# Second output projection of a two-layer decoder step, turned from feature rows to token rows

## What is computed

```python
# pool_mixer, layer 1; y is (tokens, 4096)
y = mixed * scale * silu(z)
out = y @ w_out                 # (tokens, 4096) @ (4096, 2048)
# trunk
hp = hp + op; hs = hs + os_     # residual
y_prompt = rmsnorm(hp, final_norm_w); y_sample = rmsnorm(hs, final_norm_w)
def rmsnorm(x, w):
    return x * rsqrt(mean(x * x, axis=-1) + 1e-6) * w
```

## Time and profile before

| | |
|---|---|
| timed runs | 2078.85, 2078.79, 2073.24 us; median 2078.79 |
| profiled execution | 2073.52 us |
| its span, first to last instruction | 2071.8 us |
| TensorE busy in the span | 99% |
| VectorE, ScalarE, GpSimd busy | 62%, 45%, 8% |
| mean granted TensorE clock | 0.995 of 2.4 GHz |
| HBM traffic | 283.85 MB read, 27.25 MB written |

### The profile page before, as it was taken

One profiled execution on the slowest core, in us unless ns is written; L12 is line 12 of the kernel. 1 busy time (PEld: TensorE's weight loads), 2 busy tenths in 40 slices (PEclk: granted clock), 3 DMA queues, 4 the chain that ended last, 5 costly groups with the idle time before them and its releaser, 6 DMA issues.

```text
span 2071.8 us, 51652 instructions
## 1 busy us (share of the span) xinstructions
PE 2045.3 (99%) x19451; PEld 1961.4 (95%) x19451; DVE 1277.5 (62%) x2245; ACT 936.8 (45%) x2013; POOL 168.7 (8%) x354
## 2 busy tenths in 40 slices
PE   8999999999999999999999999999999999999997
PEld 7999999999999999999899999999999999999997
DVE  5767677777677777767754445545546656644444
ACT  5555555565555555455543343333333333433333
POOL 4111111011111011111000010000000000000000
PEclk9999999999999999999999999999999999999999
DMA  6544555554455554455554445444454444454452
GB/s 201 168 132 134 162 153 153 152 145 122 140 162 162 148 151 135 124 155 156 160 168 152 143 142 182 144 158 149 148 165 151 147 147 158 158 162 144 141 161 73
DMA packets 381227, 311.13 MB, mean 150 GB/s; under 512 B 20041, under 2 KB 377114, under 8 KB 380570
## 3 DMA queue, kind: packets, MB, share of 16 engines
q1 hardware_dynamic: 379290, 306.30, 48.7%
q10 hardware_dynamic: 1872, 3.96, 0.6%
HBM read 283.85 MB, written 27.25 MB: 150 GB/s over the span
## 4 chain that ended last, share of the span: by engine, by line
PE 92%; DVE 6%; issue 1%; ACT 1%; DMA 0%; POOL 0%; DVEq 0%; ACTq 0%; POOLq 0%; SPq 0%
PE ps L298 27%; PE ps L299 25%; PE ps L300 25%; PE ps L1221 10%; DVE s_s L1154 2%; PE ps L1371 2%; DVE wlo L289 1%; DVE silu L1016 1%; DVE silu L1014 1%; DVE amat L1164 1%; PE ps L1411 0%; PE ps L1345 0%; DVE xlo L1008 0%; DMA ht<-ht_save 0%; DVE xlo L893 0%
## 5 line engine op out<-in xcount | busy, mean ns | idle before, releaser
L298 PE MATMUL ps<-xhi,whi 128*128 128x320 f32 x3072 | 983.3, 320 | 7.4 <-DVE xlo L1008 3.5
L300 PE MATMUL ps<-xhi,wlo 128*128 128x320 f32 x3072 | 949.1, 309 | 0.0
L299 PE MATMUL ps<-xlo,whi 128*128 128x320 f32 x3072 | 948.8, 309 | 0.0
L289 DVE TENSOR_TENSOR wlo<-wraw,whi 128x1024 fp32r<-128x1024 f32 (+1 forms) x484 | 596.0, 1252 | 236.6 <-ACT whi L284 234.1
L284 ACT ACTIVATE whi<-wraw 128x1024 fp32r<-128x1024 f32 (+1 forms) x484 | 498.1, 1049 | 318.7 <-PE ps L300 287.9
L298 PEld LDWEIGHTS ps<-xhi,whi 128*128 128x128 f32 x3072 | 576.9, 188 | 32.0 <-issue 17.4
L299 PEld LDWEIGHTS ps<-xlo,whi 128*128 128x128 f32 x3072 | 577.4, 188 | 0.9
L300 PEld LDWEIGHTS ps<-xhi,wlo 128*128 128x128 f32 x3072 | 576.6, 188 | 0.0
L298 PE MATMUL ps<-bhi,whi 128*128 128x320 f32 x512 | 157.6, 308 | 0.0
L299 PE MATMUL ps<-blo,whi 128*128 128x320 f32 x512 | 157.6, 308 | 0.0
L300 PE MATMUL ps<-bhi,wlo 128*128 128x320 f32 x512 | 157.6, 308 | 0.0
(11 more groups left out here) (342 smaller groups left out, 2077.4 us busy)
## 6 DMA issues: line engine op xcount, KB each, us to landing
wraw<-in_delta_w_in_dram SPq DMA_DIRECT2D x384, 256.0 KB, 3.0
wraw<-in_pool_w_in_dram SPq DMA_DIRECT2D x256, 256.0 KB, 3.0
wraw<-in_delta_w_out_dram SPq DMA_DIRECT2D x128, 256.0 KB, 3.3
wraw<-in_pool_w_out_dram SPq DMA_DIRECT2D x128, 256.0 KB, 3.2
s_s<-in_state_delta_dram SPq DMA_DIRECT2D x32, 512.0 KB, 6.3
out_dram<-s_s SPq DMA_DIRECT2D x32, 512.0 KB, 4.2
wraw<-in_pool_w_group_dram SPq DMA_DIRECT2D x64, 256.0 KB, 3.2
dec<-gc_rows SPq DMA_DIRECT2D x16, 320.0 KB, 4.1
```

The source lines that it names most:

```text
L289: nc.vector.tensor_tensor(wlo[:, slot, 0:width], wraw[:, slot, 0:width], whi[:, slot, 0:width].bitcast(F32), ALU.subtract).then_inc(E("w_l ...
L298: mm(o, whi[:, slot, w], hi[:, k_x, :], start=first, stop=False)
L299: mm(o, whi[:, slot, w], lo[:, k_x, :], start=False, stop=False)
L300: done = mm(o, wlo[:, slot, w], hi[:, k_x, :], start=False, stop=last)
```

## The change

The second output projection is done with the roles exchanged. The tokens of `branch` are stationary (128 at a time) and the weights move, 512 output columns at a time, so the result comes in token rows. There are three groups of tokens: 128 and 128 of the prompt, and the 64 of the samples. The samples' high and low parts stand side by side in one stationary tile of 128 columns (`rows_s`), so this group takes two matmuls instead of three; its low x low product comes along, and the two halves of the result (64 partitions each) are added by VectorE. A piece is now 2 input tiles x 512 columns (`two_rows`), and there are 8 steps of 8 pieces: 2 halves of the input x 4 blocks of 512 columns, with three banks a step, two sets in turn (4, 5, 6 and 0, 1, 2). In the first four steps TensorE also turns `ht` into token rows, by 12 groups of 4 transposes into banks 7 and 3 after the first three pieces of a step, and ScalarE copies them into `hrow` and `hrow_c`; VectorE adds each step's product to these rows. Squares are summed along the row by ScalarE's accumulator, one column a group and block. `final_norm_w` is loaded as one row spread over all partitions (`wrow`), and each finished block of 512 columns but the last is multiplied by it into `yrow` (`weigh`). In the last step the last four pieces are worked off group by group; after each group come its add, square, root, reciprocal, a scaling of 1536 columns on ScalarE (for the samples 896, the rest on VectorE) and of the last 512 on VectorE, and two stores. GpSimd has no part in the stage.

The steps of `out_sp`, `out_act`, `out_dve` and `out_pe` for r = 2 are taken out; for r = 1 they stay as they were. At the end of `mix` two lines change, and the last four loads of it fetch pieces of the new form:

```diff
-                    sc.activation(xhi[:, 4 * ch:4 * ch + 4, :], branch[:, 4 * ch:4 * ch + 4, :], ACT.Copy).then_inc(E("b_hi"), 1)
+                    rows_hi_part(0, ch)
...
-                    v.tensor_tensor(xlo[:, 4 * jb:4 * jb + 4, :], branch[:, 4 * jb:4 * jb + 4, :],
-                                    xhi[:, 4 * jb:4 * jb + 4, :].bitcast(F32), ALU.subtract).then_inc(E("b_lo"), 1)
+                    rows_lo_part(0, jb)
...
-            out_sp(sp, 2, OUT_B, pw_out)
+            rows_sp(sp)
...
-            out_pool(pool, 2)
...
-            out_act(act, 2, OUT_B, J_OUT_B)
+            rows_act(act)
...
-            out_dve(dve, 2, OUT_B, J_OUT_B)
+            rows_dve(dve)
...
-            out_pe(pe, 2, OUT_B, J_OUT_B)
+            rows_pe(pe)
```

The new functions:

```diff
+    F0 = J_OUT_B // 2 + 1
+    STEPS = 8
+    ROWS = ((P, 0), (P, 1), (64, 2))
+
+    ROW_SIDES = ((rows_hi0, rows_lo0, rows_s0), (rows_hi1, rows_lo1, rows_s1))
+
+    def rows_hi_part(half, ch):
+
+        hi, lo, both = ROW_SIDES[half]
+        k, src = slice(4 * ch, 4 * ch + 4), branch[:, KT * half + 4 * ch:KT * half + 4 * ch + 4, :]
+        nc.scalar.activation(hi[:, k, :], src[:, :, 0:256], ACT.Copy)
+        nc.scalar.activation(both[:, k, 0:64], src[:, :, 256:T], ACT.Copy).then_inc(E("b_hi"), 1)
+
+    def rows_lo_part(half, ch):
+
+        hi, lo, both = ROW_SIDES[half]
+        k, src = slice(4 * ch, 4 * ch + 4), branch[:, KT * half + 4 * ch:KT * half + 4 * ch + 4, :]
+        nc.vector.tensor_tensor(lo[:, k, :], src[:, :, 0:256], hi[:, k, :].bitcast(F32), ALU.subtract)
+        nc.vector.tensor_tensor(both[:, k, 64:P], src[:, :, 256:T], both[:, k, 0:64].bitcast(F32), ALU.subtract
+                                ).then_inc(E("b_lo"), 1)
+
+    def step_banks(t):
+
+        return (4, 5, 6) if t % 2 == 0 else (0, 1, 2)
+
+    def row_chunk(g, s):
+
+        c = slice(512 * s, 512 * s + 512)
+        return hrow[:, g, c] if g < 2 else hrow_c[s // 2][0:64, 512 * (s % 2):512 * (s % 2) + 512]
+
+    def sq_col(g, s):
+        return small[0:64 if g == 2 else P, 16 + 4 * g + s:17 + 4 * g + s]
+
+    def rows_sp(sp):
+        for t in range(STEPS):
+            half, s = t // 4, t % 4
+            for pc in range(8):
+                n = 8 * t + pc
+                if n < 4:
+                    continue
+                load(sp, OUT_B + n, pc % 4, two_rows(pc % 4, KT * half + 2 * pc, 512 * s))
+            if t == 4:
+                sp.wait_ge(E("w_used"), OUT_B + 32)
+                sp.dma_start(wrow[:], final_norm_w.partition_broadcast(P)).then_inc(E("rows_in"), 16)
+        y_s = y_sample.rearrange("b s c -> (b s) c")
+        for rows, g in ROWS:
+            y = y_prompt[0, P * g:P * g + P, :] if g < 2 else y_s
+            sp.wait_ge(E("dve_tiles"), len(BY_DVE) + g + 1)
+            sp.dma_start(y[:, 1536:DM], row_chunk(g, 3)).then_inc(E("rows_out"), 16)
+            sp.wait_ge(E("act_tiles"), len(BY_ACT) + g + 1)
+            sp.dma_start(y[:, 0:1536], yrow[0:rows, g, :]).then_inc(E("rows_out"), 16)
+        sp.wait_ge(E("rows_out"), 6 * 16)
+        sp.wait_ge(E("cc_dma"), 128 * NH)
+        sp.wait_ge(E("delta_out"), 48 * NH + 16)
+        sp.wait_ge(E("cp_dma"), 32 * NH + 16)
+
+    def rows_act(act):
+        sc = nc.scalar
+
+        def residual(s, g):
+
+            n = 3 * s + g
+            act.wait_ge(E("tiles_t"), KT + n + 1)
+            if n == 0:
+                act.wait_ge(E("b_lo"), 12)
+            to = row_chunk(g, s)
+            sc.activation(to, ps[0:64 if g == 2 else P, (7, 3)[n % 2], :], ACT.Copy).then_inc(E("y_tiles"), 1)
+
+        def branch_hi(ch):
+
+            if ch == 0:
+                for pair in range(2):
+                    act.wait_ge(E(f"free{pair}"), F0)
+            rows_hi_part(1, ch)
+
+        def square(g, s):
+            rows = 64 if g == 2 else P
+            return sc.activation(sqrow[0:rows, 3 * (s % 2) + g, :], row_chunk(g, s), ACT.Square, accum_out=sq_col(g, s))
+
+        for t in range(STEPS):
+            half, s = t // 4, t % 4
+            for q in range(8):
+                n = 8 * t + q + LEAD
+                if n < 8 * STEPS:
+                    split_hi(act, OUT_B + n, n % 4)
+                if half == 0 and 1 <= q <= 3:
+                    residual(s, q - 1)
+                if half == 0 and q == 5:
+                    branch_hi(s)
+                if q == 3 and t > 4:
+
+                    act.wait_ge(E(f"free{(t - 1) % 2}"), F0 + (t - 1) // 2 + 1)
+                    for rows, g in ROWS:
+                        last = square(g, s - 1)
+                    last.then_inc(E("sqp"), 1)
+        sc.activation(small[:, 63:64], ones[:, 0:1], ACT.Sqrt)
+        for rows, g in ROWS:
+            act.wait_ge(E("y_tiles"), 12 + g + 1)
+            square(g, 3).then_inc(E("sqp"), 1)
+            act.wait_ge(E("sqp"), 8 + 3 + g + 1)
+            act.wait_ge(E("ms"), 3)
+            sc.activation(small[0:rows, 32 + g:33 + g], sq_col(g, 3), ACT.Sqrt, scale=1.0 / DM,
+                          bias=small[0:rows, 28 + g:29 + g]).then_inc(E("rms"), 1)
+            act.wait_ge(E("rinv"), 3 + g)
+            act.wait_ge(E("xnorm"), KT + 3)
+            cols = 1536 if g < 2 else 896
+            sc.activation(yrow[0:rows, g, 0:cols], yrow[0:rows, g, 0:cols], ACT.Copy, scale=small[0:rows, 36 + g:37 + g]
+                          ).then_inc(E("act_tiles"), 1)
+
+    def rows_dve(dve):
+        v = nc.vector
+
+        def branch_lo(ch):
+            dve.wait_ge(E("b_hi"), 12 + ch + 1)
+            rows_lo_part(1, ch)
+
+        def add(g, t):
+
+            bank, to = step_banks(t)[g], row_chunk(g, t % 4)
+            if g < 2:
+                return v.tensor_tensor(to, ps[:, bank, :], to, ALU.add)
+            v.tensor_tensor(to, ps[0:64, bank, :], to, ALU.add).then_inc(E("zs"), 1)
+            dve.wait_ge(E("zs"), 4 * NG + t + 1)
+            return v.tensor_tensor(to, ps[64:P, bank, :], to, ALU.add)
+
+        def weigh(s):
+
+            for rows, g in ROWS:
+                c = slice(512 * s, 512 * s + 512)
+                last = v.tensor_tensor(yrow[0:rows, g, c], row_chunk(g, s), wrow[0:rows, c], ALU.mult)
+            last.then_inc(E("xnorm"), 1)
+
+        for t in range(STEPS):
+            half, s = t // 4, t % 4
+            for q in range(8):
+                n = 8 * t + q + LEAD
+                if n < 8 * STEPS:
+                    split_lo(dve, OUT_B + n, n % 4)
+                if half == 0 and q == 6:
+                    branch_lo(s)
+                if q == 4 and t > 4:
+                    dve.wait_ge(E("rows_in"), 144)
+                    dve.wait_ge(E(f"free{(t - 1) % 2}"), F0 + (t - 1) // 2 + 1)
+                    weigh(s - 1)
+                if q == 6 and t == STEPS - 1:
+
+                    dve.wait_ge(E("sqp"), 8 + 3)
+                    for rows, g in ROWS:
+                        c = slice(0, rows)
+                        v.tensor_tensor(small[c, 40 + g:41 + g], small[c, 16 + 4 * g:17 + 4 * g], small[c, 17 + 4 * g:18 + 4 * g], ALU.add
+                                        ).then_inc(E("sums"), 1)
+                        dve.wait_ge(E("sums"), 2 * NH + 2 * g + 1)
+                        v.tensor_tensor(small[c, 40 + g:41 + g], small[c, 40 + g:41 + g], small[c, 18 + 4 * g:19 + 4 * g], ALU.add
+                                        ).then_inc(E("sums"), 1)
+                        dve.wait_ge(E("sums"), 2 * NH + 2 * g + 2)
+                        last = v.tensor_scalar(small[c, 28 + g:29 + g], small[c, 40 + g:41 + g], 1.0 / DM, EPS, ALU.mult, ALU.add)
+                    last.then_inc(E("ms"), 1)
+            if t < STEPS - 1:
+                dve.wait_ge(E("w_used"), OUT_B + 8 * t + 8)
+                dve.wait_ge(E("y_tiles"), min(3 * t + 3, 12))
+                for rows, g in ROWS:
+                    last = add(g, t)
+                last.then_inc(E(f"free{t % 2}"), 1)
+
+        def finish(g, rows):
+
+            dve.wait_ge(E("rms"), 3 + g)
+            v.reciprocal(small[0:rows, 36 + g:37 + g], small[0:rows, 32 + g:33 + g]).then_inc(E("rinv"), 1)
+            dve.wait_ge(E("rinv"), 3 + g)
+            if g == 2:
+                v.tensor_scalar(yrow[0:rows, g, 896:1536], yrow[0:rows, g, 896:1536], small[0:rows, 36 + g:37 + g], None, ALU.mult)
+            v.scalar_tensor_tensor(row_chunk(g, 3), row_chunk(g, 3), small[0:rows, 36 + g:37 + g], wrow[0:rows, 1536:DM],
+                                   ALU.mult, ALU.mult).then_inc(E("dve_tiles"), 1)
+
+        for rows, g in ROWS:
+            dve.wait_ge(E("ssum"), 2 + g)
+            add(g, STEPS - 1).then_inc(E("y_tiles"), 1)
+            finish(g, rows)
+
+    def rows_pe(pe):
+        mm = nc.tensor.matmul
+
+        def turn_residual(s, g):
+
+            n = 3 * s + g
+            if n >= 2:
+                pe.wait_ge(E("y_tiles"), n - 1)
+            b = ps[:, (7, 3)[n % 2], :]
+            rows = 64 if g == 2 else P
+            for q in range(4):
```

(97 more changed lines are left out.)

43 lines of the change are left out of this document (4 added, 39 removed).

## The result

The changed kernel took 2085.69 us (median of 10 runs, 2080.16 to 2087.75), the kernel before 2078.22 (10 runs): ratio 1.0042, 95% interval 1.0032 to 1.0053: slower by 0.4%, little but clear of the noise. (The two medians alone make 1.0036.) The profiled execution has a span of 2078.4 us against 2071.8, +6.6. The profiled executions, 2080.16 and 2073.52 us, took about as little as the shortest timed ones.

The account below looks back on a forecast made before the run. The prediction took TensorE as the bound, a dense matmul stream and then a latency-bound tail; +6.8 + 5.2 - 12.7 = -0.7 us of span gave 2078.1 us, no measurable change, range 2064 to 2087.

Parts of the forecast that it names:

- 1023 spacings: Second projection's matmul stream: 1023 starts of 512-column matmuls 0.2267 us apart, 231.9 us against 225.1, +6.8.
- 48 transposes: Residual turned into token rows inside the matmul stream: 48 transposes at 0.108 us each, +5.2 us on TensorE's path.
- feeding TensorE: Splits and loads supplying the matmul stream: covered by two split pieces, 7.3 us, against VectorE's 4.1; cost 0.
- The fixed reading: Matmul stream: each matmul with its load costs 13.4 ns beside its columns, so 512 columns take 226.7 ns.
- The floor: Matmul stream: weight loads set the 146.7 ns and longer matmuls hide it; 213.3 ns each, total 2064.4 us; chance 0.22.
- proportional reading: Matmul stream: streaming 10% below a column per cycle, 234.7 ns per 512 columns, total 2086.3 us; chance 0.20.
- The tail: From the last matmul's start to the end of the span: 10.0 us against 22.66, -12.7; bounds 9 to 13.
- the case of a stall: Step ends: VectorE's adds and split, or the broadcast, hold up TensorE; 1 us at each of 7 gives 2085; chance 0.08.

Follow-up runs that it names:

- the run with both edits: Changed kernel with the last three pieces grouped instead of four and the second half's stationary tiles 32 bytes later; ratio to the kernel before 1.0002.

## Why the prediction was wrong, point by point

| term, us | forecast | measured |
|---|---|---|
| 1023 spacings | 231.9 | 231.9, and 3.4 for the second half's place |
| 48 transposes | 5.2 | 5.4, and some 0.3 behind them |
| feeding TensorE | 0 | 4.2 |
| first to last matmul | 237.1 | 245.2 |
| last matmul to the end | 10.0 | 8.95 |
| change of the span | -0.7 | +6.6 |

**Feeding** is the step that failed. It weighed VectorE's work at the step ends against two split pieces in hand, and that was right: no wait stands there. It did not follow the last step's change of order. With four pieces by group, TensorE waits for the splits of all four before the first product, so it wants the split of piece 63 right after piece 59; and ScalarE may write that split only when piece 59 is used. The cover of two pieces, counted correctly for the steady stream, is nothing there. With three pieces by group the wait is gone. 2.56 us of gap, the rest of the 4.2 from the lower clock behind it.

**The spacing.** The fixed reading was right, and exactly: 13.3 ns beside the columns at 512 as at 320, wherever the two operands lie at the same place. The floor fell. The size was off for half the matmuls by 6.7 ns, a cost of placement that the trace before could not show, as 320-column matmuls don't have it. Its mechanism inside the chip stays open. It looked like half of the proportional reading, but that one gives 0.2347 for both halves. The rule of the Trainium skill ("TensorE: Matmul & The Clock Gate", Back-to-back issue gap), which that section gives for an isolated matmul, would make 0.2158; no stretch went at it.

**The tail** was sized well, 1.05 us too long. The timeline of it, to be read against the terms:

```profile
2069.88 0.68 DVE L2048 TENSOR_TENSOR hrow_c<-ps,hrow_c 64x512 f32<-64x512 f32 x1 [0.98 <-PE ps L2130]
2070.60 0.69 DVE L2050 TENSOR_TENSOR hrow_c<-ps,hrow_c 64x512 f32<-64x512 f32 x1
2071.33 0.63 ACT L2004 ACTIVATE sqrow<-hrow_c 64x512 f32<-64x512 f32 x1 [1.59 <-DVE hrow_c L2050]
...
2072.08 0.29 ACT L2028 ACTIVATE small<-small 64x1 f32<-64x1 f32 x1
2072.41 0.16 DVE L2094 RECIPROCAL small<-small 64x1 f32<-64x1 f32 x1 [1.11 <-ACT small L2028]
...
2072.60 0.55 DVE L2097 TENSOR_SCALAR yrow<-yrow,small 64x640 f32<-64x640 f32 x1
2073.07 0.74 DVE L2098 SCALAR_TENSOR_TENSOR hrow_c<-hrow_c,small,wrow 64x512 f32<-64x512 f32 x1
2073.83 0.55 SPq L1975 DMA_DIRECT2D out_dram<-hrow_c  x1
2074.42 0.59 SPq L1977 DMA_DIRECT2D out_dram<-yrow  x1
```

Adds, square and root are as forecast, with no table load between. Scaling 640 columns took 0.55, not 0.72, and from the last issue to the end are 4.0 us, not 4.65.

**The verdict.** Without the two unforeseen costs the stage would have come out as written: the run with both edits has 237.54 and 8.95 us where 237.1 and 10.0 stood, and measures as no change. The changed kernel's time lies in the range by way of two costs that none of its cases had: the case of a stall was worked out for the wrong place, with a chance of 0.08, and placement was no case at all.

## What to carry to other kernels

When a change alters the order in which pieces are used, check at the point of change what the last needed piece waits for: a lead that is enough in the steady order can be none where several pieces are waited for at once, and the clock can add to the gap (here some 1.2 us, in two traces of three). Put the two operands of 512-column four-byte matmuls at the same place modulo 512 bytes; here it was 3% of their time, for a 32-byte shift. Exchanging the operands' roles moved 20 us into the stream to take 14 out of the tail: count columns and transposes in the dense part first.

## What the runs showed of the hardware

A placement cost of 5.7 to 7.6 ns a matmul that belongs to the pair of operands, not to one, at 512 columns and not at 320 (the table above). A gap of 2.56 us was followed by some 3 us at half the clock in two traces and by none in a third.

And a source of the runs' spread, by their granted clock. At the end of the first layer TensorE has one idle time of 1.44 us between small matmuls, in both traces shown below; the profile names no releaser for it. In six of the 18 profiles the clock is 0.93 on average from 1030 to 1100 us, and the stage starts at 1828.8 to 1831.7 us; in one it is 0.95, and the stage starts at 1827.1; in the other eleven it is 1.00, and the stage starts at 1823.7 to 1825.6. The kernel before's profile is one of the eleven, the run with both edits one of the six, and their code is the same there. Two windows of the kernel before:

```profile
1048.00:1056.00 8.00, 8.00 (x62) 7.51 (x61) 3.73 (x8) 4.08 (x8) 0.00 (x0) 1.00 0.45 134
1056.00:1064.00 8.00, 8.00 (x57) 6.91 (x56) 4.90 (x12) 3.00 (x13) 2.26 (x2) 1.00 0.58 208
```

The same windows of the run with both edits:

```profile
1048.00:1056.00 8.00, 6.66 (x54) 5.75 (x55) 4.41 (x8) 2.91 (x7) 0.00 (x0) 0.64 0.22 69
1056.00:1064.00 8.00, 8.00 (x42) 7.76 (x41) 2.44 (x7) 1.82 (x3) 0.00 (x0) 0.72 0.21 66
```

Clocks of 0.64 and 0.72 over 8 us each lose 5.1 us of full speed (0.36 x 8 + 0.28 x 8), about the distance between the two clusters of the runs of before (2073 and 2078 us). What decides whether the clock falls there isn't shown.
